# A sixth resident slot for expert weights, laid over the normalised tokens and the first ring slot

## The reference, cut to what matters

```python
def _hier_moe(x, w_rg, b_rg, w_re, b_re, w_gate, w_up, w_down):
    # top-1 group of 4, then top-2 of its 8 experts; every token uses 2 of 32 experts
    ...
    for e in range(N_EXPERTS):
        h = jax.nn.silu(xt @ w_gate[e]) * (xt @ w_up[e])
        y = y + combine[:, e:e + 1] * (h @ w_down[e])
```

## Time and profile before

| | us |
|---|---|
| median of 3 runs (lowest to highest) | 2249.31 (2247.08 to 2257.26) |
| the profiled execution | 2237.74 |
| its span | 2236.0 |
| TensorE (PE) busy in the span | 2055.1 (92%) |
| VectorE, ScalarE, GpSimd busy | 1187.9, 692.9, 743.4 |
| weight queue of SyncE (q1) | 254.35 MB, 30.2% of 16 DMA engines |

### The profile page before, as it was taken

The page is one execution under the profiler, slowest core; times in us unless marked ns, Lnnn a source line. Parts: engine busy times, 40 slices in busy tenths (PEclk is TensorE's granted clock), DMA queues, the critical chain, the costliest instruction groups (busy, mean ns, idle before and its releaser), DMA issues.

```text
span 2236.0 us, 24957 instructions
## 1 busy us (share of the span) xinstructions
PE 2055.1 (92%) x8468; PEld 1325.8 (59%) x8469; DVE 1187.9 (53%) x1968; ACT 692.9 (31%) x1230; POOL 743.4 (33%) x1218
## 2 busy tenths in 40 slices
PE   7999889999998999889999999999998897987885
PEld 5865468888786874367888786454333445333332
DVE  6546766678546446777678644236872524111113
ACT  4328734334323217834334322120001501101010
POOL 0306766756201006776666300004660001111110
PEclk9999999999999999999999999999999997999998
DMA  4210022232233210022333222122331133799984
GB/s 172 85 41 1 39 94 104 104 113 98 87 103 112 94 50 1 38 85 94 104 104 115 85 92 94 64 88 94 113 113 57 79 147 155 320 423 423 424 319 156
DMA packets 44259, 284.19 MB, mean 127 GB/s; under 512 B 8394, under 2 KB 8650, under 8 KB 21632
## 3 DMA queue, kind: packets, MB, share of 16 engines
q1 hardware_dynamic: 34272, 254.35, 30.2%
q0 software_dynamic: 9024, 19.08, 2.2%
q10 hardware_dynamic: 864, 9.44, 1.0%
HBM read 272.68 MB, written 23.60 MB: 133 GB/s over the span
## 4 chain that ended last, share of the span: by engine, by line
PE 78%; DVE 8%; DMA 7%; ACT 3%; POOL 2%; issue 2%; SPq 0%; DVEq 0%; POOLq 0%; ACTq 0%
PE bank L808 11%; PE bank L810 10%; PE bank L809 10%; DMA experts<-in_experts 6%; PE bank L1058 5%; PE bank L1232 4%; PE bank L992 3%; PE bank L993 3%; PE bank L994 3%; PE bank L1028 2%; PE bank L1163 2%; PE bank L928 2%; PE bank L899 2%; PE bank L1235 2%; PE bank L915 1%
## 5 line engine op out<-in xcount | busy, mean ns | idle before, releaser
L808 PE MATMUL bank<-h_high,w_high 128*128 128x512 f32 x1056 | 418.0, 396 | 39.3 <-ACT h_high L1597 13.7
L809 PE MATMUL bank<-h_low,w_high 128*128 128x512 f32 x1056 | 414.9, 393 | 0.0
L810 PE MATMUL bank<-h_high,w_low 128*128 128x512 f32 x1056 | 414.8, 393 | 0.0
L1465 ACT ACTIVATE w_high<-extra 128x2048 fp32r<-128x2048 f32 (+1 forms) x104 | 180.6, 1737 | 347.3 <-DVE w_low L1868 347.2
L1865 DVE TENSOR_SCALAR extra<-ring 128x2048 int32<-128x2048 int32 (+1 forms) x104 | 116.9, 1124 | 262.7 <-PE bank L810 137.6
L808 PEld LDWEIGHTS bank<-h_high,w_high 128*128 128x128 f32 x1056 | 201.0, 190 | 92.0 <-issue 27.3
L810 PEld LDWEIGHTS bank<-h_high,w_low 128*128 128x128 f32 x1056 | 200.6, 190 | 42.7
L809 PEld LDWEIGHTS bank<-h_low,w_high 128*128 128x128 f32 x1056 | 201.2, 190 | 41.3
L1868 DVE TENSOR_TENSOR w_low<-ring,extra 128x2048 fp32r<-128x2048 f32 (+1 forms) x104 | 217.3, 2090 | 3.6
L1232 PE MATMUL bank<-experts,rstd 128*64 128x512 f32 x512 | 129.2, 663 | 29.2 <-DMA experts<-in_experts 28.5
L993 PE MATMUL bank<-act_low,w_high 128*128 128x512 f32 x352 | 139.0, 395 | 0.0
(11 more groups left out here) (434 smaller groups left out, 3691.7 us busy)
## 6 DMA issues: line engine op xcount, KB each, us to landing
experts<-in_experts SPq DMA_DIRECT2D x34, 2048.0 KB, 24.1
ring<-in_w_ffn_in SPq DMA_DIRECT2D x44, 1024.0 KB, 4.8
experts<-in_experts SPq DMA_DIRECT2D x34, 1024.0 KB, 21.8
ring<-in_w_ffn_out SPq DMA_DIRECT2D x32, 704.0 KB, 4.0
ring<-in_w_feature SPq DMA_DIRECT2D x14, 1024.0 KB, 4.8
ring<-in_w_rest SPq DMA_DIRECT2D x9, 1024.0 KB, 4.9
ring<-in_w_out SPq DMA_DIRECT2D x8, 1024.0 KB, 4.9
powers_d<-work POOLq DMA_DIRECT2D x16, 512.0 KB, 3.1
```

What stands on the lines that cost most here:

```text
L808: pe.matmul(dst, high[:, at], h_high[:, k, :], start=k == 0, stop=False)
L809: pe.matmul(dst, high[:, at], h_low[:, k, :], start=False, stop=False)
L810: return pe.matmul(dst, low[:, at], h_high[:, k, :], start=False, stop=k == KD - 1)
L1465: act.activation(w_high[par_][:, 0:words], w_part[par_][:, 0:words], ACT.Copy).then_inc(w_split, 1)
```

## The change

One more slot for expert weights, `FIXED_SLOTS` = 6, is used for the 32 regular loads. The sixth, `last_slot`, is a second name for memory that exists: it begins where `h` begins and spans `h` and the first 2048 words behind it, all of `ring[0]`. Expert e goes to slot e % 6. Expert 5, the first in the new slot, waits for `hrows_out` >= 80 (all five stores landed, so that `h` and `ht` have been read) instead of `gated`; later ones wait with e - 6 in place of e - 5. The second output buffer `yo[1]` lay in `ring[0]`; it moves to the second half of `ring[1]`. TensorE takes its operands through `expert_part`, which is evaluated while the program is written. The repeated loads behind pair 15 keep their five slots and their waits.

```diff
+FIXED_SLOTS = EXPERT_SLOTS + 1
...
+        (last_slot,) = second_names(("last_slot", [P, EXPERT_WORDS], F32))
         h = sb("h", [P, KD, T])
...
-        xg, yo = [ring[2][:, 0:D], ring[1][:, 0:D]], [ring[2][:, D:2 * D], ring[0][:, 0:D]]
+        xg, yo = [ring[2][:, 0:D], ring[1][:, 0:D]], [ring[2][:, D:2 * D], ring[1][:, D:2 * D]]
+
+        def expert_part(e, lo, n):
+            slot = e % FIXED_SLOTS
+            return last_slot[:, lo:lo + n] if slot == EXPERT_SLOTS else experts[:, slot * EXPERT_WORDS + lo:slot * EXPERT_WORDS + lo + n]
...
             def load_expert(e):
-                slot = e % EXPERT_SLOTS
-                at = slot * EXPERT_WORDS
-                if e >= EXPERT_SLOTS:
-                    sp.wait_ge(gated, (e - EXPERT_SLOTS) // 2 + 1)
-                sp.dma_start(experts[:, at:at + KD * 2 * DE], a["experts"][e, :, 0:KD * 2 * DE]).then_inc(expert_in[slot], 16)
-                if e >= EXPERT_SLOTS:
-                    sp.wait_ge(down_done, 2 * ((e - EXPERT_SLOTS) // 2 + 1))
-                sp.dma_start(experts[:, at + KD * 2 * DE:at + EXPERT_WORDS], a["experts"][e, :, KD * 2 * DE:])\
-                  .then_inc(expert_down_in[slot], 16)
+                slot = e % FIXED_SLOTS
+                if e >= FIXED_SLOTS:
+                    sp.wait_ge(gated, (e - FIXED_SLOTS) // 2 + 1)
+                elif slot == EXPERT_SLOTS:
+                    sp.wait_ge(hrows_out, 16 * (NQ + 1))
+                sp.dma_start(expert_part(e, 0, KD * 2 * DE), a["experts"][e, :, 0:KD * 2 * DE]).then_inc(expert_in[slot], 16)
+                if e >= FIXED_SLOTS:
+                    sp.wait_ge(down_done, 2 * ((e - FIXED_SLOTS) // 2 + 1))
+                sp.dma_start(expert_part(e, KD * 2 * DE, 2 * D), a["experts"][e, :, KD * 2 * DE:]).then_inc(expert_down_in[slot], 16)
 
             sp.wait_ge(pe_done, done2("w_out2", KD - 1))
-            for e in range(EARLY_EXPERTS, EXPERT_SLOTS):
-                load_expert(e)
-            for e in range(EXPERT_SLOTS, NE):
+            for e in range(EARLY_EXPERTS, NE):
                 load_expert(e)
...
-                        pe.wait_ge(expert_in[e % EXPERT_SLOTS], 16 * (e // EXPERT_SLOTS + 1))
+                        pe.wait_ge(expert_in[e % FIXED_SLOTS], 16 * (e // FIXED_SLOTS + 1))
...
-                            o = (2 * p + s) % EXPERT_SLOTS * EXPERT_WORDS + k * 2 * DE
                             ins = pe.matmul(bank[2][s * ROWS:(s + 1) * ROWS, :], xgt[:, k * P + s * ROWS:k * P + (s + 1) * ROWS],
-                                            experts[:, o:o + 2 * DE], start=k == 0, stop=k == KD - 1)
+                                            expert_part(2 * p + s, k * 2 * DE, 2 * DE), start=k == 0, stop=k == KD - 1)
```

More of the change, by code:

```diff
@@ L613, in build @@
         spare_zero = sem("spare_zero")
-        expert_in = [sem(f"expert_in{n}") for n in range(EXPERT_SLOTS)]
-        expert_down_in = [sem(f"expert_down_in{n}") for n in range(EXPERT_SLOTS)]
+        expert_in = [sem(f"expert_in{n}") for n in range(FIXED_SLOTS)]
+        expert_down_in = [sem(f"expert_down_in{n}") for n in range(FIXED_SLOTS)]
         more_in = sem("more_in")
@@ L1250, in down @@
                     for e in (2 * p, 2 * p + 1):
-                        pe.wait_ge(expert_down_in[e % EXPERT_SLOTS], 16 * (e // EXPERT_SLOTS + 1))
+                        pe.wait_ge(expert_down_in[e % FIXED_SLOTS], 16 * (e // FIXED_SLOTS + 1))
                 else:
@@ L1259, in down @@
                             for s in range(2):
-                                o = (2 * p + s) % EXPERT_SLOTS * EXPERT_WORDS + w
                                 ins = pe.matmul(bank[5 + hf][s * ROWS:(s + 1) * ROWS, :], hgt[:, k * P + s * ROWS:k * P + (s + 1) * ROWS],
-                                                experts[:, o:o + T], start=k == 0, stop=k == 1)
+                                                expert_part(2 * p + s, w, T), start=k == 0, stop=k == 1)
                         else:
```

## The result

| | before | changed |
|---|---|---|
| median of 5 runs (lowest to highest), us | 2254.88 (2247.08 to 2257.59) | 2236.11 (2234.80 to 2240.17) |
| ratio, 95% interval | | 0.9944 (0.9921 to 0.9966) |
| profiled execution, its span, us | 2237.74, 2236.0 | 2234.80, 2233.1 |

The first comparison says 0.56% faster. The mean of the three is 0.9961. The forecast was -0.33%, ratio 0.9967; it lies just outside the first interval, which ends at 0.9966, and inside the other two. The ratios are what is compared here.

A forecast was written before the change was run, and what follows sets the result against it. The second block's expert stage was taken as bound by its weight transfers; one expert's 7.42 us off the median 2249.31, all other terms 0, gave 2241.9 us (-0.33%), range 2235 to 2250.

The forecast's parts named there:

- The bound: Second block's experts: weight transfers limit the stage, DMA busy share 1.01 at 424 GB/s from 1950.70 to 2117.40.
- the moved buffer: Output buffer yo[1] moved to ring slot 1's second half: same copies, scatters and waits, cost 0.
- The early load: Expert 5 issued at 1888.3, streaming 1889.9 to 1897.4 inside the idle DMA gap; collision with the first gather taken as 0.
- rival 1: Before pair 0: early load's tail overlaps the first gather, costing 1 to 6.5 us, time 2243 to 2248.4; chance 0.13.
- The term of the sum: Saturated queue after the restart: one expert fewer, 3 MB at 424 GB/s, last landing 7.42 us earlier.
- The wait: Added wait for hrows_out on SyncE: only expert loads from 6 on stand behind it, not due until 1913.38; nobody delayed.
- the look-ahead: Six slots lengthen the queue in front of TensorE but not the bytes; gathers keep some 22 us: 0.
- Rival 3: Gap before pair 0 not used: expert 5 goes out only at about 1913, time stays 2249.3; chance 0.03.
- Rival 4: Saturated stretch: deeper queue recovers 1.8 us or slower runs lose time there; gain 7.8 to 9.6 us, chance 0.13.
- What follows pair 15: Extra-expert loads and the remaining chain move along with the last landing, nothing given back while 6.1 us of slack last.
- the bounds of the costs: Range for the whole kernel from the bounds of the costs alone: 2239.7 to 2248.4 us.
- rivals 2 and 3: The first of these: early load fully delays the first gather and TensorE's clock stays low, +3.6 us, 2252.9 us; chance 0.03.

The follow-up runs named there:

- the three: The changed kernel measured three times against the kernel before, without further edit: ratios 0.9944, 0.9965 and 0.9975.
- two halves: Changed kernel with gate and up parts of experts 6 and 7 in halves, the first issued after half of pair 0's gate matmuls; ratio 0.9948 against the kernel before.
- four quarters: Changed kernel with gate and up parts of experts 6 and 7 issued in quarters during pair 0's gate matmuls; ratios 0.9922 and 0.9953 against the kernel before.
- the fill: Changed kernel plus 19 purposeless matmuls in TensorE's pauses before the lists and first transposes: ratio 0.9981 against the kernel before; with four quarters also, 0.9960.

## Why the prediction was right, and where it was off

**The bound.** Right. The stage is bound by the queue before and after: busy share 1.01 in both, and taking bytes out of it moves the landing by those bytes (5.0 us for 2 MB, 7.2 for 3 MB, and 0 for none, even with six slots and the moved buffer).

**The early load.** Issue 27.6 us after the mark (27.9 forecast), end at 1904.0 - 7.05 = 1896.95 on the old scale (1897.4 forecast), first gather 3.38 us (3.5). The margin was as thin as I gave it, under 1 us: the load ends as the gather is issued. In all three profiles of the changed kernel the gather took 3.38 to 3.50 us, so rival 1 did not occur. Moved 8 us later, the load costs the gather 5.3 us, inside rival 1's bounds of 1 to 6.5.

**The term of the sum.** 7.42 us was forecast for one expert; the flow got shorter by 7.48 in the first pair of profiles and by 7.2 in the mean of three against four. The price by 424 GB/s holds. The whole stage is 8.2 us shorter in the same means (366.9 against 375.1); the 1 us beyond the flow lies in the lengths of pair 0 and pair 15, which vary with the clock. At the 358 GB/s of the Trainium skill (HBM Reference, Specifications) the estimate was 8.8, and no run shows it.

**The wait, the moved buffer, the look-ahead.** 0 each, and the runs show 0: 0.9998 for the buffer alone and 1.0012 for six slots without the early load, with flows of 221.77 and 221.30. Rival 3, the unused gap, fell with the row of `last_slot` at 1895.11 in SyncE's queue. Rival 4's 1.8 us, from a fuller first stretch, did not come: the stretch after the restart runs at 404 GB/s in the changed kernel too. Its other half, that slower executions lose time in the saturated stretch, did not show either: among the kernels without an early load, the flow is 221.3 and 221.8 us with the mark at 1868.55 and 1869.64, and 221.4 with it at 1860.44.

**What follows pair 15.** "The whole rest moves along": nearly. The extra weights kept a slack, 4.5 us instead of 6.1 (SyncE goes on at 2140.79, they are needed at 2145.30). The stretch is 100.5 us against 101.2. One wait is new and was not in the prediction: TensorE waits 0.65 us to turn the rows of the second extra step, for a gather issued at 2142.13, which takes 10.82 us beside the weights. In the kernel before its slack was small: issued at 2145.80, up to 10.0 us for such a gather, used from 2155.95 on. Neither belongs to the change alone: in the second profile of the changed kernel pair 15's gate matmuls took 8.45 us instead of 7.09, the stretch is 101.04 us, and the wait is absent.

**The time.** 2241.9 us was forecast from a median of 2249.31 over three runs. The median of the kernel before became 2254.88 over five runs and was 2246.02 over the 35 runs of a later comparison. The changed kernel had 2236.11, then 2238.41 and 2237.98 over 12 runs each. So the level I started from was right only to some microseconds. The first pair of medians is 18.8 us apart, two and a half times the 7.4 forecast, the later pairs 7.6 and 9.0; that the 2236.11 lies near the forecast time confirms the term less than the flows do. The first ratio, 0.9944, is 0.23% below the forecast one with 0.22% of uncertainty. I had left 0.17 for a gain of over 0.5%, for scatter alone; the first comparison fell there, the two larger ones inside 0.5%. One working was incomplete: the bounds of the costs, 2239.7 to 2248.4, leave out the prediction's own rivals 2 and 3, at 2252.9 and 2249.3; neither came. What I missed was that much of the scatter lies in few places ahead of the change. Windows of TensorE's clock from 900 to 1000 us, hundreds of microseconds ahead of anything the change touches (columns: window, length, PE busy, granted clock, DMA share, GB/s), in the kernel before, the changed kernel, and the run with the load beside the gather:

```profile
900.00:1000.00 100.00, 88.02 (x402) 0.97 0.18 67
```

```profile
900.00:1000.00 100.00, 90.19 (x402) 0.92 0.16 58
```

```profile
900.00:1000.00 100.00, 91.70 (x375) 0.80 0.13 48
```

The end of the last projection in these three is 1860.44, 1867.49 and 1877.54. Over the fourteen profiles it lies between 1858.5 and 1878.9 whatever was changed behind it. That is 20 us, nearly three times the effect. This stretch is not the only place: the run with two halves has 0.97 in it and its mark still at 1867.10, but its clock is 0.89 from 200 to 400 us, where the kernel before has 0.96. Why the clock is lower there in some executions is not settled here.

## What to carry to other kernels

Where a saturated queue ends last, a change is worth the bytes that it moves into time in which the queue was idle, at the queue's own rate. The number of slots and the depth of the look-ahead were worth nothing by themselves here. Don't count on the full rate in small parts or at a start: at the restart, four quarters gained 3.6 us of the 7.4 expected. Look for the idle stretch ahead of the flow first, and check which small transfer on the path ends it: here a load 8 us later gave back 5 of 7 us. To read an effect of a third of a per cent from profiles, mark the point ahead of which nothing has changed and compare from there.

## What the runs showed of the hardware that was not expected

- TensorE's granted clock makes the same instructions differ between executions: pair 0's 32 gate matmuls took 8.4 to 8.7 us in seven profiles, 9.32 in one and 10.05 to 10.07 in four of the twelve without the fill, in changed and unchanged kernels alike, and 7.09 after the fill. The Trainium skill (TensorE: Matmul & The Clock Gate, Part 1) says that the number of matmuls at the lower level at a start differs from run to run of one kernel; the trace agrees.
- A gather of 128 rows takes 3.4 us alone and 8.75 beside a 3 MB load.
- A busy share near 1 of the DMA engines doesn't mean 420 GB/s: they moved 279 GB/s at 0.98 for 2 us amid 512 KB parts issued in pairs, and 287 at 1.00 in the first 2 us of a 2 MB load, where 418 went with 0.98 in a running flow. The cause is not shown.
